# A hybrid decoder layer on one core: the order of the 24 matmuls of a weight panel

## What is computed

```python
h = concatenate([meta, x])
xn = rmsnorm(h, norm1_g)
proj = xn @ w_in          # columns: attention q, k, v, forget gate; conv B, C, h;
                          # linear attention q, k, v, r, low-rank gate; three merge gates
ya = forgetting_attention(qa, ka, va, logf) @ w_a_o
yb = (sc_b * causal_dwconv(sc_c * sc_h, conv_w)) @ w_b_o
yc = (silu(rc) * rmsnorm(gated_linear_attention(qc, kc, vc, logg))) @ w_c_o
mix = sigmoid(g_a + b_a) * ya + sigmoid(g_b + b_b) * yb + sigmoid(g_c + b_c) * yc
h = h + mix @ w_o
u_gate, u_up = split(causal_dwconv(rmsnorm(h, norm2_g) @ w_up, mlp_conv_w))
h = h + (silu(u_gate) * u_up) @ w_down
out = rmsnorm(h, final_norm_g)[:, 16:]
```

## Time and profile before

| | |
|---|---|
| median of 3 runs | 1746.43 us (1746.4 to 1746.43) |
| profiled execution, first to last instruction (span) | 1745.1 us |
| TensorE busy with matmuls | 1734.3 us, 13,429 matmuls |
| VectorE / ScalarE / GpSimd busy | 1117.8 / 763.7 / 263.3 us |
| HBM read | 311.10 MB, 179 GB/s over the span |

### The profile page before, as it was taken

The page is one execution under the profiler, slowest core; times in us unless marked ns, Lnnn a source line. Parts: engine busy times, 40 slices in busy tenths (PEclk is TensorE's granted clock), DMA queues, the critical chain, the costliest instruction groups (busy, mean ns, idle before and its releaser), DMA issues.

```text
span 1745.1 us, 34098 instructions
## 1 busy us (share of the span) xinstructions
PE 1734.3 (99%) x13429; PEld 1680.7 (96%) x13429; DVE 1117.8 (64%) x1607; ACT 763.7 (44%) x921; POOL 263.3 (15%) x494
## 2 busy tenths in 40 slices
PE   9999999999999999999999999999999999999998
PEld 8999999999999999999999999999999999888886
DVE  6857766667565554555556687777777777554454
ACT  6635444354354444444444444334444444343433
POOL 3153332630530000000000043321000000000000
PEclk9999999999999999999999999999999999999999
DMA  8567557666565655556645566666555565665654
GB/s 232 169 180 186 168 149 198 176 175 178 153 184 181 189 178 178 175 182 194 201 159 192 181 195 192 204 200 192 183 182 181 180 186 180 223 190 189 189 192 134
DMA packets 310296, 320.62 MB, mean 184 GB/s; under 512 B 17353, under 2 KB 285133, under 8 KB 310093
## 3 DMA queue, kind: packets, MB, share of 16 engines
q1 hardware_dynamic: 296861, 311.01, 58.2%
q0 software_dynamic: 12928, 7.80, 2.0%
q10 hardware_dynamic: 432, 0.79, 0.1%
HBM read 311.10 MB, written 2.11 MB: 179 GB/s over the span
## 4 chain that ended last, share of the span: by engine, by line
PE 99%; DVE 0%; DMA 0%; ACT 0%; SPq 0%; issue 0%; ACTq 0%; DVEq 0%
PE ps L1435 27%; PE ps L1437 27%; PE ps L1436 27%; PE ps L1693 5%; PE ps L1692 5%; PE ps L1691 5%; PE ps L1526 0%; DMA xb<-in_x_dram 0%; PE ps L1540 0%; PE ps L1565 0%; PE ps L1555 0%; PE ps L1556 0%; PE ps L1584 0%; PE ps L1585 0%; DVE xl L941 0%; DVE lo L896 0%
## 5 line engine op out<-in xcount | busy, mean ns | idle before, releaser
L896 DVE TENSOR_TENSOR lo<-raw,hi 128x1024 fp32r<-128x1024 f32 x584 | 709.9, 1229 | 494.4 <-ACT hi L627 490.2
L1435 PE MATMUL ps<-xh,hi 128*128 128x260 f32 (+1 forms) x3328 | 945.8, 284 | 0.2 <-DVE xl L941 0.2
L1437 PE MATMUL ps<-xh,lo 128*128 128x260 f32 (+1 forms) x3328 | 941.7, 283 | 0.0
L1436 PE MATMUL ps<-xl,hi 128*128 128x260 f32 (+1 forms) x3328 | 936.5, 281 | 0.0
L627 ACT CAST hi<-raw 128x1024 fp32r<-128x1024 f32 x584 | 604.8, 1048 | 671.8 <-PE ps L1437 539.0
L1436 PEld LDWEIGHTS ps<-xl,hi 128*128 128x128 f32 x3328 | 626.6, 188 | 0.2
L1435 PEld LDWEIGHTS ps<-xh,hi 128*128 128x128 f32 x3328 | 625.2, 188 | 1.3 <-issue 0.4
L1437 PEld LDWEIGHTS ps<-xh,lo 128*128 128x128 f32 x3328 | 624.7, 188 | 0.0
L610 POOL DMA_DIRECT2D hT<-h2b x128 | 69.6, 553 | 604.3 <-DVE h2b L1289 599.7
L1693 PE MATMUL ps<-lo,act_h 128*128 128x512 f32 x350 | 138.5, 396 | 0.0
L1692 PE MATMUL ps<-hi,act_l 128*128 128x512 f32 x350 | 137.3, 392 | 0.0
(11 more groups left out here) (298 smaller groups left out, 1383.6 us busy)
## 6 DMA issues: line engine op xcount, KB each, us to landing
raw<-in_w_in_dram SPq DMA_DIRECT2D x224, 512.0 KB, 3.6
raw<-in_w_up_dram SPq DMA_DIRECT2D x176, 512.0 KB, 4.6
raw<-in_w_down_dram SPq DMA_DIRECT2D x88, 512.0 KB, 4.7
raw<-in_w_o_dram SPq DMA_DIRECT2D x32, 512.0 KB, 3.4
raw<-in_w_in_dram SPq DMA_DIRECT2D x32, 256.0 KB, 4.2
raw<-in_w_a_o_dram SPq DMA_DIRECT2D x16, 512.0 KB, 4.3
raw<-in_w_b_o_dram SPq DMA_DIRECT2D x16, 512.0 KB, 3.3
raw<-in_w_c_o_dram SPq DMA_DIRECT2D x16, 512.0 KB, 3.3
```

The source lines that it names most:

```text
L896: nc.vector.tensor_tensor(part(ph, i, q, lo_all), raw[:, s, :], part(ph, i, q, hi_all).bitcast(F32), ALU.subtract).then_inc(lo_ready, 1)
L1435: nc.tensor.matmul(acc, w_hi, mh, start=first and j == 0, stop=False)
L1436: nc.tensor.matmul(acc, w_hi, ml, start=False, stop=False)
L1437: ins = nc.tensor.matmul(acc, w_lo, mh, start=False, stop=last and j == KJ - 1)
```

## The change

A new function, `use_turns`, issues a panel's 24 matmuls in another order: for each output block `m`, first high weights by high tokens for four rows, then high weights by low tokens for four rows, then low weights by high tokens for four rows, the rows each time as 0, 3, 1, 2. It serves every panel of GT, WO and UP, and those of BR save pair 3 and the two with transposes between their halves (the first two panels of the program). Those, and the down projection, are as before.

```diff
--- before.py
+++ after.py
@@ -1420,6 +1420,20 @@
 
         @block.tensor
         def _(pe):
+            KINDS = ((hi, 0), (hi, 1), (lo, 0))
+            IN_TURNS = [(m, j, kind) for m in range(2) for kind in range(3) for j in (0, 3, 1, 2)]
+
+            def use_turns(ph, i, q, st, moving, n, first, last):
+
+                pe.wait_ge(lo_ready, ph.panel(i, q) + 1)
+                s = ph.slot(q)
+                for at, (m, j, kind) in enumerate(IN_TURNS):
+                    weights, side = KINDS[kind]
+                    begins, ends = at % (3 * KJ) == 0, at % (3 * KJ) == 3 * KJ - 1
+                    ins = nc.tensor.matmul(pset(st, n)[:, m, :], tiles(weights, s, j, m), moving(j)[side],
+                                           start=first and begins, stop=last and ends)
+                ins.then_inc(panel_used, 1)
+
             def use_panel(ph, i, q, st, moving, n, first, last, skip=0, between=None):
 
                 pe.wait_ge(lo_ready, ph.panel(i, q) + 1)
@@ -1619,7 +1633,10 @@
                         pe.wait_ge(gstat_inv, i)
                     a, n = window[pair]
                     between = (lambda c: lambda: input_chunk(c))(q + 2) if i == 0 and q < 2 else None
-                    use_panel(BR, i, q, st, x_window((q % 4) * KJ, a, n), n, q % 4 == 0, q % 4 == 3, C0 if pair == 3 else 0, between)
+                    if pair == 3 or between:
+                        use_panel(BR, i, q, st, x_window((q % 4) * KJ, a, n), n, q % 4 == 0, q % 4 == 3, C0 if pair == 3 else 0, between)
+                    else:
+                        use_turns(BR, i, q, st, x_window((q % 4) * KJ, a, n), n, q % 4 == 0, q % 4 == 3)
                     if i == 0 and q < SCQ:
                         first_branch(q)
                     if q >= SCQ:
@@ -1645,7 +1662,7 @@
                     if first and q == 12:
                         pe.wait_ge(oa_lo, BR.trips)
                         pe.wait_ge(pads_zero, 6)
-                    use_panel(GT, i, q, st, mv, NC, kq == 0, kq == last)
+                    use_turns(GT, i, q, st, mv, NC, kq == 0, kq == last)
                     if first and q < SCQ:
                         mixers(BR.trips - 1, q + MXQ)
 
@@ -1660,7 +1677,7 @@
                     if kq == 0:
                         pe.wait_ge(set_free[st], i + WO_SET[st])
                     pe.wait_ge(mix_lo, 2 * kq + 2)
-                    use_panel(WO, i, q, st, (lambda k0: lambda j: (mix_h[:, k0 + j, C0:T], mix_l[:, k0 + j, C0:T]))(kq * KJ),
+                    use_turns(WO, i, q, st, (lambda k0: lambda j: (mix_h[:, k0 + j, C0:T], mix_l[:, k0 + j, C0:T]))(kq * KJ),
                               NC, kq == 0, kq == 3)
 
 
@@ -1671,7 +1688,7 @@
                         pe.wait_ge(set_free[st], i + UP_SET[st])
                     if first:
                         pe.wait_ge(h2_lo, 2 * kq + 2)
-                    use_panel(UP, i, q, st, x_window(kq * KJ, C0, NC), NC, kq == 0, kq == 3)
+                    use_turns(UP, i, q, st, x_window(kq * KJ, C0, NC), NC, kq == 0, kq == 3)
                     if first and q == 1:
                         pe.wait_ge(h2sq_sum, KT)
                         nc.tensor.matmul(AUX[0][:, 0:NQ], ones[:], sqsum[:, 0:NQ], start=True, stop=True).then_inc(r2_ps, 1)
```

## The result

The changed kernel takes **1748.99 us** (median of 18 runs, 1748.34 to 1750.65); the kernel before, on the same chips, 1746.55 us (18 runs, 1746.21 to 1748.36). The ratio is 1.0015 with a 95% interval of 1.0008 to 1.0021: 2.4 us slower. Forecast were 7 us less.

What follows compares the result with a forecast made beforehand. TensorE's matmul steps were taken to bound the kernel; 0.6 ns less on 11,472 matmuls saves 6.9 us, so the span goes from 1745.1 to 1738.2 us, plus 1.3 us around it gives 1739.5 us; range 1730 to 1757 us.

Steps and rivals of the forecast that it cites:

- What bounds the kernel: Whole kernel: TensorE, 99% of the chain, sets the time by how fast one matmul follows another; other engines aren't late.
- the price of the new step: Reordered panels: start-to-start time of successive matmuls falls from 118.9 to 118.3 ns; 11,472 matmuls save 6.9 us.
- the two kinds that load a different weight tile: Old panels: steps L1436 to L1437 (both tensors change), 117.6 ns, and L1437 to L1435 (weights change tensor, next row), 119.0 ns.
- the dearest kind: Old panels: step L1435 to L1436, same high weight tile loaded a second time, 120.1 ns; it disappears with the change.
- The rival "slower": Reordered panels: row jumps put streams in a bad relation, costing 0.7 ns a matmul, 8.0 us, giving 1754.4 us; chance 25%.
- The rival "no change": Reordered panels: the overhead belongs to the stream, so order doesn't alter the mean step; 1746.4 us; chance 28%.
- The Trainium skill's rule: Matmul steps: columns over 2.4 GHz plus about 2.5 ns, 110.8 ns, whatever goes before; order would gain 0 us.

Runs made afterwards that it cites:

- The best order found here: Kernel before, reordered panels with rows 0, 1, 2, 3 at 260 columns and 0, 3, 1, 2 at 272, kinds in groups of four: 1739.82 us, ratio 0.9961.
- nudge: One of six small float32 matmuls (16 to 128 columns) added between the last panels of the first gates trip; on the kernel before 1748.33 us, on the changed kernel 1743.78.

## Why the prediction was wrong

*What bounds the kernel* was right. TensorE is 99% of the span in every run here, it took no new wait, the other engines stayed covered (in the changed kernel VectorE idles 490.9 us for ScalarE, before it 490.2), and each change of the step went into the span. The untouched parts held: 11.09 us for 48 steps of the down projection, and pair 3, from its second panel to the panel behind its last, takes 8.84 us as in the earlier trace rows:

```profile
58.04 0.28 PE L1449 MATMUL ps<-xh,hi 128*128 128x260 f32 x1
...
66.88 0.66 PE L1433 MATMUL ps<-xh,hi 128*128 128x272 f32 x4
```

*The step that failed* is the price of the new step: "I take the mean of the two kinds that load a different weight tile, (117.6 + 119.0)/2 = 118.3 ns, because these are the kinds of which the new order is made, and the dearest kind is the one that disappears." The 120.1, 117.6 and 119.0 ns of the earlier trace rows are means over a pattern of 24 steps, sorted by a label that doesn't cause them. Two signs were in the trace. In the down projection the dear step follows L1692 in the first stretch of the earlier trace rows (238 ns) and L1693 in the second (235 ns); I used these rows only for their mean. And the two halves of a panel, which have the same twelve pairs of row and kind, had different steps, so row and kind together don't fix a step's length. The runs put the sequence of the token rows in its place: with the kinds in turns and the new rows the counts are those of the new order, 120.0 ns in the gates, and with the kinds exactly as in the kernel before and only the rows' order changed the step is 119.7 instead of 118.9. That 118.3 ns is also what the up-projection shows is an accident of two numbers, and no support.

*The rival "slower"* had the mechanism that the runs bear out, streams that begin "in another relation" to the last, but took it as one price for all reordered matmuls. It is +1.1 ns in some phases and -0.6 in another, so its 1754.4 us was too high. That pair 3 is a case of the same thing wasn't tested.

*The rival "no change"* named a total 2.6 us from the measured one, by a reason that is false: the overhead is not a fixed property of the stream. By order alone, the steady step of 260 columns ran from 118.3 to 120.5 ns in the phases behind the branches. The result lies inside its 0.2%, because a gain of 2.3 us in the up-projection takes back half of a loss of 4.4 us in the gates and the mixture product; that is luck, not support.

*The Trainium skill's rule* in "TensorE: Matmul & The Clock Gate", section "Back-to-back issue gap", has columns and clock only. My prediction left out that the section gives it for isolated matmuls, and says that in a stream of weight loads and matmuls both set the distance. Taken as a price of a stream it gave the better total here, and these runs contradict it as a law: the same 192 matmuls of 260 columns take 22.72 or 23.04 us at the same granted clock of 1.00. Nor is what a step has over its columns at 2.4 GHz a fixed sum: 118.3 - 108.3 = 10.0 ns with 260 columns, 231.1 - 213.3 = 17.8 with the down projection's 512.

*The range* of 1730 to 1757 us held the result (it stops short of the 1758.4 us that it was meant to reach); the chances, 0.47 for faster and 0.28 for no change, did not favour it.

What stays open: what in the chip makes the rhythm, and which property of an interruption chooses between 118.3 and 120.0 ns. The weight loads stand as closely one behind the other as the matmuls do, and no run changes their length or number, so whether the rhythm needs them isn't known.

## What to carry to other kernels

When one engine's instructions run back to back and their distances are uneven, look for the period of the unevenness before pricing it by kind; if the period is longer than the list of kinds, or moves between kinds in code that didn't change, it is a rhythm, and only its mean counts. On a kernel that is all matmuls, the order of the moving operand's rows is worth a search: several orders can be tried in one run, a phase each, and read from the counts of matmuls in a stretch. The best order found here is worth 0.4%. Prefer an order that shows one rate behind every interruption over one that shows two, and don't judge an order by its total alone, since here the total hid +1.1 ns in one phase and -0.6 in another.

## What the runs showed of the hardware

- A chain of float32r matmuls with nothing to wait for can run at several steady rates with the same code: 118.3 and 120.0 ns a step for rows 0, 3, 1, 2, and in the branches 119.2, 120.0 and 121.7 ns for 0, 2, 1, 3. It holds its rate for hundreds of microseconds, through 4000 matmuls, and changes it where another matmul interrupts it.
- The steps follow the start addresses of the moving operand's rows, modulo 256 bytes: with 1152 bytes between rows the sequences 0, 2, 1, 3 and 0, 3, 1, 2 have the same four steps (117.6, 122.4, 121.0, 119.0 and 117.3, 122.6, 120.9, 119.1 ns), with 1088 bytes they don't. The stationary operand's places had no effect in the one run that moved them (119.2 ns either way), and which of the high and low tensors is used had none with rows 0, 3, 1, 2 (the same counts in all four stretches).
- An interruption costs its first step and little more in the old order: behind a nudge the first step is 203 or 204 ns, the panel's other 22 take 119.2 on average, beside the steady 118.9.
